# The tables of turns of a state space layer, made one stage earlier in a kernel of six blocks

## The reference, cut to what matters

```
def swiglu(h, w_gate_up, w_down):              # (1024 -> 2*2816), (2816 -> 1024)
    g, u = split(h @ w_gate_up, 2)
    return (silu(g) * u) @ w_down

def s5_layer(h, w_in, a_re, a_im, log_dt, b, c, d, w_glu):
    u = h @ w_in                               # 64 groups of 16 channels
    lam_bar = exp(lam * dt)                    # 64 groups x 64 complex states
    bu = einsum('gpc,bsgc->bsgp', b_bar, u_g)  # b_bar = (lam_bar - 1) / lam * b
    states = associative_scan(s[t] = lam_bar * s[t-1] + bu[t])
    y = real(einsum('gcp,bsgp->bsgc', c, states)) + d * u
    val, gate = split(gelu(y) @ w_glu, 2)
    return val * sigmoid(gate)
```

## Time and profile before

| | |
|---|---|
| median of 3 runs | 3997.28 us (3992.02 to 3998.29) |
| profiled execution | 3999.34 us, span 3997.6 us, mean granted clock 0.949 |
| TensorE products busy | 3683.6 us (92%) |
| VectorE busy | 2068.0 us (52%) |
| ScalarE busy | 1080.4 us (27%) |
| GpSimd busy | 1069.7 us (27%) |

### The profile page before, as it was taken

One profiled execution on the slowest core, in us unless ns is written; L12 is line 12 of the kernel. 1 busy time (PEld: TensorE's weight loads), 2 busy tenths in 40 slices (PEclk: granted clock), 3 DMA queues, 4 the chain that ended last, 5 costly groups with the idle time before them and its releaser, 6 DMA issues. The chain is left out here.

```text
span 3997.6 us, 44371 instructions
## 1 busy us (share of the span) xinstructions
PE 3683.6 (92%) x16819; PEld 2874.8 (72%) x16819; DVE 2068.0 (52%) x2631; ACT 1080.4 (27%) x1480; POOL 1069.7 (27%) x835
## 2 busy tenths in 40 slices
PE   7889999968999979999889999997899999779999
PEld 6667888846788848887666888762678877357887
DVE  4446554795544475444445545655543346454334
ACT  3442121123212122213442212333222223332121
POOL 0443634610554236340342635001200000130000
PEclk9889999978999989999889999987999999889999
DMA  3105444123444324442113444210133321013332
GB/s 103 48 27 127 129 124 116 58 66 75 125 131 129 107 81 131 125 116 83 44 32 100 127 127 119 81 35 21 43 95 100 88 82 56 21 32 84 93 101 79
DMA packets 554319, 346.08 MB, mean 87 GB/s; under 512 B 33270, under 2 KB 535420, under 8 KB 554172
## 3 DMA queue, kind: packets, MB, share of 16 engines
q1 hardware_dynamic: 540348, 293.79, 26.1%
q0 software_dynamic: 13824, 50.34, 4.3%
HBM read 341.01 MB, written 3.08 MB: 86 GB/s over the span
## 5 line engine op out<-in xcount | busy, mean ns | idle before, releaser
L1273 PE MATMUL ps<-h_hi,w_hi 128*128 128x512 f32 x2880 | 1154.2, 401 | 50.9 <-DVE qk L1840 17.8
L1274 PE MATMUL ps<-h_lo,w_hi 128*128 128x512 f32 x2880 | 1136.7, 395 | 0.0
L1275 PE MATMUL ps<-h_hi,w_lo 128*128 128x512 f32 x2880 | 1135.6, 394 | 0.0
L1235 DVE TENSOR_TENSOR w_lo<-w,w_hi 128x2048 fp32r<-128x2048 f32 (+2 forms) x294 | 663.4, 2257 | 168.0 <-ACT w_hi L1228 165.9
L1228 ACT ACTIVATE w_hi<-w 128x2048 fp32r<-128x2048 f32 (+2 forms) x294 | 507.0, 1725 | 708.4 <-PE ps L1275 635.1
L1273 PEld LDWEIGHTS ps<-h_hi,w_hi 128*128 128x128 f32 x2880 | 551.1, 191 | 172.3 <-issue 56.2
L1275 PEld LDWEIGHTS ps<-h_hi,w_lo 128*128 128x128 f32 x2880 | 549.6, 191 | 117.7
L1274 PEld LDWEIGHTS ps<-h_lo,w_hi 128*128 128x128 f32 x2880 | 551.4, 191 | 110.7 <-issue 0.5
L1364 DVE TENSOR_TENSOR sg<-sg,ps 128x512 f32<-128x512 f32 x132 | 90.8, 688 | 719.3 <-ACT sg L1349 719.3
L1273 PE MATMUL ps<-a_hi,w_hi 128*128 128x512 f32 x1056 | 412.0, 390 | 0.0
L1275 PE MATMUL ps<-a_hi,w_lo 128*128 128x512 f32 x1056 | 411.0, 389 | 0.0
(11 more groups left out here) (471 smaller groups left out, 3990.1 us busy)
## 6 DMA issues: line engine op xcount, KB each, us to landing
w<-in_ffn_w_gate_up SPq DMA_DIRECT2D x176, 512.0 KB
w<-in_w_ada POOLq DMA_DIRECT2D x96, 512.0 KB, 6.9
w<-in_ffn_w_down SPq DMA_DIRECT2D x64, 704.0 KB
w<-in_w_gate_up SPq DMA_DIRECT2D x88, 512.0 KB
w<-in_w_down SPq DMA_DIRECT2D x32, 704.0 KB
w<-in_fox_w_in SPq DMA_DIRECT2D x32, 512.0 KB
w<-in_w_in SPq DMA_DIRECT2D x14, 1024.0 KB
w<-in_fox_w_in SPq DMA_DIRECT2D x8, 1024.0 KB
```

Of the source, the lines that this page charges most:

```text
L1235: last = nc.vector.tensor_tensor(lo, raw, hi.bitcast(F32), ALU.subtract)
L1273: nc.tensor.matmul(out, hi, a[0][:, k, :], start=k == 0, stop=False)
L1274: nc.tensor.matmul(out, hi, a[1][:, k, :], start=False, stop=False)
L1275: return nc.tensor.matmul(out, lo, a[0][:, k, :], start=False, stop=k == kt - 1)
```

## The change

The tables leave `S5Mix` and become the side work of the second `SplitDown` of the first feed-forward, in the chunks 0 to 6. They lie now in arena tiles 8 to 15 (`h_lo`), with tiles 0 and 1 (`h_hi`) for intermediate results; both are free once `SplitGateUp` is done. u and what shares its tiles moves to tiles 16 to 23, and `s5_low` to tile 8. The arithmetic is the same, but that the last doubling of the angle, after the table of 32, is left out. As the second `SplitDown` now has a side, its chunks are written out for TensorE and ScalarE.

```diff
-        self.s5_low = at("s5_low", 16 * S, [P, DK, S], F32R)
+        self.s5_low = at("s5_low", 8 * S, [P, DK, S], F32R)
...
-        self.ut = at(8, 4096).rearrange("p (g a c) -> p g a c", a=4, c=C5)
+        self.ut = at(16, 4096).rearrange("p (g a c) -> p g a c", a=4, c=C5)
...
-        self.ec, self.es = at(16, 2048), at(20, 2048)
+        self.ec, self.es = tables.ec, tables.es
...
         weights(0)
         for q in range(3):
             block(q)
         weights(1)
-        turns()
-        for n in (1, 2, 4, 8):
-            table(n)
         weights(2)
-        table(16)
         block(3)
         block(4)
         block(5)
         keep(0)
-        table(32)
         block(6)
...
+class S5Tables:
+    def __init__(self, m, prep):
+        self.m, self.sm = m, prep.sm
+        flat = m.arena[:, :]
+        self.ec, self.es = (flat[:, t * S:(t + 4) * S] for t in (8, 12))
+        self.etmp = flat[:, 0:1024]
+    def vector(self, e, j):
...
+        def cosines(n):
+            t = three(self.etmp[:, 0:32 * n], n)
+            wc, ws = wide(sm["cs"], n), wide(sm["sn"], n)
+            do(tt(ec[:, :, n:2 * n], ec[:, :, 0:n], wc, ALU.mult))
+            do(tt(t, es[:, :, 0:n], ws, ALU.mult))
+            do(tt(ec[:, :, n:2 * n], ec[:, :, n:2 * n], t, ALU.subtract))
...
+        def double():
+            do(tt(sm["t"], sm["cs"], sm["cs"], ALU.mult))
+            do(tt(sm["k"], sm["sn"], sm["sn"], ALU.mult))
+            do(stt(sm["sn"], sm["sn"], 2.0, sm["cs"], ALU.mult, ALU.mult))
+            do(tt(sm["cs"], sm["t"], sm["k"], ALU.subtract))
+        if j == 0:
+            for x in range(3):
+                double()
+                do(tt(sm["er"], sm["er"], sm["er"], ALU.mult))
+            nc.vector.memset(ec[:, :, 0:1], 1.0)
+            do(nc.vector.memset(es[:, :, 0:1], 0.0))
+        for n in {1: (1, 2), 2: (4,), 3: (8,), 4: (16,)}.get(j, ()):
+            cosines(n)
+            sines(n)
+            double()
+        if j == 5:
+            cosines(32)
+        if j == 6:
+            sines(32)
...
-        parts += [SplitGateUp(m, gate_up, half, None if half else norm, ada), SplitDown(m, down, half, gate, None if half else side, final)]
+        parts += [SplitGateUp(m, gate_up, half, None if half else norm, ada), SplitDown(m, down, half, gate, sides[half], final)]
...
-               units=l * 2 * (FH_K + 1), side=prep if l == 0 else None, final=l == 3)
+               units=l * 2 * (FH_K + 1), sides=(prep, tables) if l == 0 else (None, None), final=l == 3)
```

More of the change, by code:

```diff
@@ L731, with __init__ @@
     late = True
-    def __init__(self, m, w, norm, prep):
+    def __init__(self, m, w, norm, prep, tables):
         super().__init__(m)
@@ L740, in __init__ @@
         self.ug = at(0, 4096).rearrange("p (g c) -> p g c", c=S5_CH)
-        self.ut = at(8, 4096).rearrange("p (g a c) -> p g a c", a=4, c=C5)
-        self.y = [at(8 + 2 * i, 1024)[0:S5_CH].rearrange("p (j n) -> p j n", j=S5_L) for i in range(2)]
-        self.st = [[at(12 + i, 256, 256 * a).rearrange("p (r c) -> p r c", r=4) for a in range(2)] for i in range(2)]
-        self.rot = [at(14, 256, 256 * i) for i in range(4)]
-        self.ec, self.es = at(16, 2048), at(20, 2048)
+        self.ut = at(16, 4096).rearrange("p (g a c) -> p g a c", a=4, c=C5)
+        self.y = [at(16 + 2 * i, 1024)[0:S5_CH].rearrange("p (j n) -> p j n", j=S5_L) for i in range(2)]
+        self.st = [[at(20 + i, 256, 256 * a).rearrange("p (r c) -> p r c", r=4) for a in range(2)] for i in range(2)]
+        self.rot = [at(22, 256, 256 * i) for i in range(4)]
+        self.ec, self.es = tables.ec, tables.es
         self.wt = [at(24 + i, S) for i in range(3)]
@@ L751, in __init__ @@
         self.taps = [at((58, 60, 66)[i], 1024).rearrange("p (g n) -> p g n", g=8) for i in range(3)]
-        self.etmp = at(68, 1024)
         sg = m.sg[:, :, :, :].rearrange("p a b s -> p (a b s)")
@@ L978, in vector @@
         self.norm.vector(e)
-        wide = lambda a, n: a.rearrange("p (i a) -> p i a", a=1).broadcast_to([P, 32, n])
-        three = lambda a, n: a.rearrange("p (i a) -> p i a", a=n)
         half = m.c("half").rearrange("p (r g c) -> p r g c", r=4, g=2)
@@ L1011, in keep @@
             last.then_inc(m.sem["k_ready"], 1)
[L1013 to L1038, removed]
         weights(0)
@@ L1532, in end, with sync, tensor, scalar @@
         finish(self.m, c_loaded=32, s5_loaded=16 * 5, s5_rows=1, turned=1, s5_step=2, s5_act=2, c_turned=2, ct_ready5=2)
+class S5Tables:
[4 more added lines that the diff above has]
+        self.etmp = flat[:, 0:1024]
+    def sync(self, e): pass
+    def tensor(self, e, j): pass
+    def scalar(self, e, j): pass
+    def end(self): pass
+    def vector(self, e, j):
+        m, nc, sm = self.m, self.m.nc, self.sm
+        tt, stt = nc.vector.tensor_tensor, nc.vector.scalar_tensor_tensor
+        do = lambda ins: m.dve(e, ins)
+        three = lambda a, n: a.rearrange("p (i a) -> p i a", a=n)
+        wide = lambda a, n: a.rearrange("p (i a) -> p i a", a=1).broadcast_to([P, 32, n])
+        ec, es = three(self.ec, S5_CH), three(self.es, S5_CH)
+        def cosines(n):
[4 more added lines that the diff above has]
+            do(tt(ec[:, :, n:2 * n], ec[:, :, n:2 * n], t, ALU.subtract))
+        def sines(n):
+            t = three(self.etmp[:, 0:32 * n], n)
+            wc, ws = wide(sm["cs"], n), wide(sm["sn"], n)
+            do(tt(es[:, :, n:2 * n], es[:, :, 0:n], wc, ALU.mult))
+            do(tt(t, ec[:, :, 0:n], ws, ALU.mult))
+            do(tt(es[:, :, n:2 * n], es[:, :, n:2 * n], t, ALU.add))
+        def double():
[17 more added lines that the diff above has]
+            sines(32)
 class SplitDown(Split):
@@ L2998, in build, with swiglu @@
             m.resume(ends)
-def swiglu(m, out, gate_up, down, norm, gate=None, units=None, side=None, final=False):
+def swiglu(m, out, gate_up, down, norm, gate=None, units=None, sides=(None, None), final=False):
     parts = []
@@ L3016, in plan @@
     prep = S5Prep(m)
+    tables = S5Tables(m, prep)
     for l in range(4):
@@ L3025, in plan @@
         elif l == 1:
-            s5 = S5Mix(m, d["s5_w_in"][0], PlaceNorm(m, lambda k, l=l: m.col("mix", 8 * l + k)), prep)
+            s5 = S5Mix(m, d["s5_w_in"][0], PlaceNorm(m, lambda k, l=l: m.col("mix", 8 * l + k)), prep, tables)
             glu = SplitGlu(m, d["s5_w_glu"][0])
```

## The result

The changed kernel takes 3964.89 us (median of 4 runs, 3959.08 to 3967.06), the kernel before beside it 3994.65 (4 runs, 3987.78 to 3998.29): ratio 0.9928 [0.9914, 0.9942], 29.8 us less. The forecast was 17.6 us less and 3980, with a range that ends at 3970. The sign was right and the largest term too, the size was not.

A forecast was written before the change was run, and what follows sets the result against it. TensorE, busy 92%, was taken as the bound, gaining only where it waits for VectorE's tables. Stalls 4.1 and clock 3.4 (7.5 us) less 25.1 give -17.6: 3981.7 from the profiled execution, 3980 against the median, range 3970 to 3989.

The forecast's parts named there:

- The bound: Behind the layer's fourth input chunk TensorE waits 24.4 us for VectorE, held by tables; removing them moves everything up 25.1 us.
- Rival 3: In the layer, something else holds the gathers; only 13.16 + 3.79 us return, less 7.5: 3988 us, chance 0.07.
- The gathers: The layer's eight gathers were left at their present 9.5 us, unslowed beside GpSimd because they read PSUM alone.
- The bound beside it: In the layer, an unslowed block(6) and TensorE at high clock through the transposes give some 3 us more: 28 us.
- 2.3 feared: Ahead of the first gather, block(6) takes two operations beside GpSimd at 1.15 us each.
- The projection's stalls: In the last projection before the layer, VectorE's table work exceeds its free time per chunk and holds TensorE 4.1 us.
- the clock's: In the projection, two larger stalls each drop TensorE to 1.2 GHz for 3.4 us: 3.4 us in all, 0 to 6.8.
- rival 1: In the projection, stalls don't disturb the clock: cost 4.1 us instead of 7.5, time 3976 us, chance 0.18.
- Rival 2: Less gained: slower gathers beside GpSimd (+4) or longer low clock in the projection (+3.4): 3984 to 3987 us, chance 0.19.
- forecast's own bounds: Layer and projection together: best 28 - 4 = 24 us gained, worst 21 - 11 = 10.
- the rival of slower gathers: In the layer, four gathers slowed beside GpSimd at ratio 2.3 cost 4.4 us more, leaving 21 us; part of rival 2.
- The rule on ports: For gathers beside GpSimd: by the skill's first half the gain stays 25 us, by its part on copies 21 us.

The follow-up runs named there:

- e6: The kernel before, tables still in the layer, with GpSimd's work there replaced by two memsets a round (other output): 3978.14 us, one execution.
- e4: The changed kernel without turns and tables, two memsets filling them with constants (a bound only, other output): 3967.86 us, ratio 0.994 to the kernel before.
- e5: The changed kernel with dead VectorE operations added in the second projection, five in chunk 2, three each in chunks 3 and 4: 3966.56 us, one execution.
- e1: The kernel before, unchanged, measured again: 3995.52 us against 3993.49, ratio 1.0003.
- e2: The changed kernel, unchanged, measured again in a later set: 3971.9 us, ratio 0.995 to the kernel before.
- e8: e7 with block(6) moved from ahead of the gathers to behind them: 3970.82 us, ratio 0.9938 to the kernel before.
- e9: The changed kernel with three starting doublings moved to the first projection's side and table operations dealt singly to the second's chunks: 3960.06 us, ratio 0.9919 to the kernel before.
- e10: e9 with block(6) moved behind the gathers: 3964.03 us, ratio 0.9924 to the kernel before.
- e3: The kernel before with an empty side in the second projection, so its chunks are written out: 3996.92 us, ratio 1.0006.
- e7: The changed kernel with tables 1 to 16 spread over projection chunks 1 to 6 and that of 32 back in the layer: 3969.04 us, ratio 0.9942 to the kernel before.

## Why the prediction was right and where it was wrong

**The bound was read rightly.** All three waits in the earlier trace rows ended where the tables' place in VectorE's order said. The chunks' end and the first gather stood 30.1 us apart before and stand 4.5 apart now; the forecast was 5.0 (801.9 to 806.9), 0.5 too many. Rival 3, in which the gathers are held by something else, falls with the wait of 2.12 us.

**The gathers were mis-sized.** I left them "at what they take now, 831.96 to 841.42, 9.5 us". By the gather and the scans' start in the table they and what stands behind them (`block(7)`, `keep(1)`) take 12.2 us in before and 10.6 in after; the gathers alone take 7.9 us (810.76 to 818.68). The 9.5 us came from a stretch with a mean clock of 0.78, which is 1.00 in after: here the stage that waits less ran at a higher clock, and I had halved `turn_w(2)`, `taps(3)` and the first two groups of transposes for it, but not the transposes behind the first gather. The bound beside it gave some 3 us for this and a faster `block(6)`; 1.5 came, and `block(6)` took 1.88 us of the 2.3 feared. Another 1.3 us come in the scans (84.0 us to 82.7), of which the forecast said nothing. They don't come from the new places of the tiles, as e6 has the old ones and takes 82.2; what gives them stays open.

**The projection's stalls were sized rightly**: 4.1 us forecast, 3.5 measured (after against e4, 75.62 and 72.09; 3.6 is taken below). The two stalls in after's timeline hold most of it: two steps from product to product, 691.83 to 693.83, take 2.0 us there instead of twice 0.23, 1.5 us more, and the other stall is as long. The prices of the earlier trace rows held (0.19, 0.43 and 0.69 us on 32, 256 and 512 columns), and 64 and 128 columns took 0.23 and 0.29 us.

**The step that failed is the clock's**: "I expect each of the two larger stalls to drop it to 1.2 GHz for 3.4 us", 3.4 us of time in all. It cost 0: PEclk stayed at 1.00 in the projection in all three traces of after, and in e5 through pauses of up to 3.34 us. The two places of the earlier trace rows had a pause of the same length, but I misread them as places in a dense stream. TensorE's timeline of before around the first of them:

```profile
1832.54 1.02 PE L397 MATMUL ps<-mean_w,acc 128*128 128x1 f32 x8 [0.30 <-PEq L2971]
1833.43 0.81 PE L293 MATMUL ps<-pastb,identb 128*128 128x512 bf16 x3
1835.83 1.76 PE L404 MATMUL ps<-diag,ones 128*128 128x128 f32 x8 [1.60 <-DVE diag L423]
1837.38 3.87 PE L293 MATMUL ps<-pastb,identb 128*128 128x512 bf16 x12
```

Both are in a norm: one-column products, a few others, then the pause and small products, where in the projection there are full chunks on both sides. That this is what takes the clock down was not tried; that the pause alone does not, e5 shows. This was rival 1, with 0.18, right in its mechanism but not in its 3976. Rival 2 falls with it, as far as it was made of a longer low clock.

**The start of the layer's chunks** is the one term I did not have. They start at 70.5 us in one trace of before and at 72.0 in another, since TensorE runs at 1.2 GHz for longer in some executions: from the first product for line 404 to the first chunk the mean PEclk is 0.76 in before (735.79 to 743.03 us) and 0.61 in e1 (736.34 to 745.05). The same fifteen products of the norm in before and in e1, the same kernel:

```profile
739.05 4.14 PE L293 MATMUL ps<-pastb,identb 128*128 128x512 bf16 x15
```
```profile
739.59 5.62 PE L293 MATMUL ps<-pastb,identb 128*128 128x512 bf16 x15
```

In the kernel before that is absorbed, the gather is at 159.43 in both, as VectorE was late anyway. In after it is not: take 3.6 us of stalls from 75.62, 75.61 and 74.11, and 72.0 and 70.5 are left. With VectorE off the path, chance in the clock there comes through to the end, 1.5 us of it and more behind (3.3 at the layer's end).

**Together**, the forecast's sum against the traces of before and after at the layer's end:

| | forecast | measured |
|---|---|---|
| stalls | +4.1 | +3.6 |
| clock in the projection | +3.4 | 0 |
| start of the layer's chunks, by chance | 0 | +1.5 |
| chunks' end to first gather, and the waits | -25.1 | -25.6 |
| gathers to scans | 0 | -1.5 |
| scans to the layer's end | 0 | -1.3 |
| sum | -17.6 | -23.3 |

So 5.7 us of the miss are terms of the sum: 3.4 for the clock, 1.5 for the gathers, 1.3 for the scans, 0.5 each for the stalls and the waits, less 1.5 for the start of the chunks. The 23.3 us lie inside the forecast's own bounds of 10 to 24.

The other 6.5 us of the first result's 29.8 are outside of the layer. In the two traces the stage between 2700 and 2880 us is 6.0 us shorter in after; but it is 6.2 us shorter in e1 too, which is the kernel before, and 2.2 in e2. That part is chance. One far difference is steadier: the stage from 1860 to 2110 us is 3.4 to 3.7 us shorter in all three traces of after and in e5, e8, e9 and e10. It is 0.5 and 1.1 us longer in e1 and e3, 0.7 longer in e6, and in e4 and e7 only 0.7 and 0.15 us shorter, and no edit lies there. Whether the earlier start of that stage or chance gives it stays open.

**The range** ends at 3970 because 2 to 3 us were allowed beyond the layer and for the medians. The first result needed 9.1: the 6.5 us above, and 2.6 because the kernel before measured 3994.65 beside it and not 3997.28, the base of the sum. So it was the allowance for chance, and not a bound of the two terms, that put the time outside. The medians of the same changed kernel lie between 3964.9 and 3971.9, and one of them is inside the range, two are not. A slip stands in the chances too: 0.50, 0.18, 0.19 and half of 0.07 make 0.905 for faster, not 0.92.

**The rule on ports.** The gathers beside GpSimd take 1.72 us for four, as without it, so the rival of slower gathers falls. The Trainium skill (SBUF — State Buffer, "Who interferes with whom") says that a VectorE instruction with two SBUF inputs contends with GpSimd's reads of SBUF and one with at most one doesn't unless it enters a two-port mode: by that rule, the trace of e6 agrees with its first half (15.0 us against 42.7), and the gathers, which read PSUM alone, show no contention. One tile of input in SBUF is no safeguard by itself: the four operations of line 423 took 3.06 us beside GpSimd's operations and 1.29 us beside its memsets.

## What to carry to other kernels

Move work to where its engine has free time and the engine that it contends with is idle too: the same operations cost nearly three times less without GpSimd's work beside them (15.0 us against 42.7). Deal them out one by one to the free time of each chunk, by prices from the trace; in e9 even the small stalls vanished. And if a stage stops waiting, price what is left of it at the higher clock as well, but charge a lower one to a pause only from a row whose surroundings are those of the pause.

## What the runs showed of the hardware

- Pauses of 1.3 to 3.3 us between full chunks of 128x512 products left TensorE at 2.4 GHz (e5, PEclk 1.00 over 73 us), while in the earlier trace rows it ran at about half the clock behind a pause of 1.6 us.
- Single executions of the kernel before differ by up to 20 us (3983.6 to 4003.3), and the largest difference between two traces of the kernel before is the granted clock of one stage (0.84 and 0.89, 6.2 us).
- The slowing goes both ways: GpSimd's own operation on two SBUF operands takes 2.28 to 2.37 us beside VectorE's table of 32 and 1.42 and 1.41 beside its copies out of PSUM (e7).
- Small operations suffered most: on 128x32 they took from 0.19 to 1.45 us while GpSimd worked (before, 768 to 811 us), where one on 128x1024 went from 1.22 (e6) to 2.07 us (e7).
- VectorE's `diag` operations, with one tile of input in SBUF, took 3.06 us for four beside GpSimd's operations (before) and 1.29 us beside its memsets (e6).
